# Result stores from ScalarE's queue, two late experts side by side on 128 partitions, and additions behind the last gated product

## What is computed

```python
def hierarchical_moe(h, ...):
    ...
    combine = ...          # (tokens, 16): the weights of each token's two experts, zero elsewhere
    gate = jnp.einsum('nd,edf->nef', h, w_gate)      # d = 1024, f = 512
    up = jnp.einsum('nd,edf->nef', h, w_up)
    act = jax.nn.silu(gate) * up * combine[..., None].astype(h.dtype)
    return jnp.einsum('nef,efd->nd', act, w_down)

def finish_layer(x, ...):
    ...
    y = hierarchical_moe(h, ...)
    return x + y.reshape(B, L, D)

y_prompt = rms_norm(xp, norm_final)
y_sample = rms_norm(xs, norm_final)
```

## Time and profile before

| | us |
|---|---|
| median of 3 runs | 888.52 (888.23 to 888.59) |
| the profiled execution, its own time | 887.74 |
| its span, first to last instruction | 886.1 |
| TensorE busy | 777.9 (88% of the span) |
| mean granted TensorE clock | 0.948 of full |
| DMA queue of SyncE | 154.16 MB |
| DMA queue of ScalarE | 5.86 MB |
| DMA queue of GpSimd | 10.30 MB |

### The profile page before, as it was taken

The page is one execution under the profiler, slowest core; times in us unless marked ns, Lnnn a source line. Parts: engine busy times, 40 slices in busy tenths (PEclk is TensorE's granted clock), DMA queues, the critical chain, the costliest instruction groups (busy, mean ns, idle before and its releaser), DMA issues.

```text
span 886.1 us, 12369 instructions
## 1 busy us (share of the span) xinstructions
PE 777.9 (88%) x4711; PEld 411.0 (46%) x4711; DVE 375.5 (42%) x869; ACT 224.4 (25%) x577; POOL 57.0 (6%) x87
## 2 busy tenths in 40 slices
PE   5988999999995889779788897799999999998457
PEld 2455465546544335345435464345455455554212
DVE  5421013571203655746755655373244333231062
ACT  1211110112202355565565641001010011100012
POOL 0111000200000000100000000200000000000220
PEclk9998999999996799999999999799999999999869
DMA  8256925173249600000000235886999999999832
GB/s 303 72 162 181 318 70 178 48 248 108 75 136 279 250 1 2 1 1 24 1 1 24 96 130 203 264 315 228 367 397 385 392 383 386 381 390 393 309 122 97
DMA packets 86381, 171.13 MB, mean 193 GB/s; under 512 B 9978, under 2 KB 25562, under 8 KB 86290
## 3 DMA queue, kind: packets, MB, share of 16 engines
q1 hardware_dynamic: 77698, 154.16, 49.1%
q0 software_dynamic: 3296, 10.30, 3.4%
q10 hardware_dynamic: 5328, 5.86, 1.9%
HBM read 151.00 MB, written 21.39 MB: 195 GB/s over the span
## 4 chain that ended last, share of the span: by engine, by line
PE 55%; issue 9%; DVE 7%; ACT 6%; DMA 3%; POOLq 0%; POOL 0%; ACTq 0%; DVEq 0%
PE bank L2294 15%; PE bank L2730 7%; PE bank L1685 6%; PE bank L2285 5%; PE bank L1620 4%; PE bank L2712 3%; PE bank L2328 3%; ACT reg L1116 3%; PE bank L1639 2%; DVE st L1277 2%; PE bank L2421 2%; ACT work L2584 1%; PE bank L2417 1%; PE bank L1622 1%; PE bank L1666 1%
## 5 line engine op out<-in xcount | busy, mean ns | idle before, releaser
L2730 PE MATMUL bank<-reg 128*128 128x512 f32 (+1 forms) x384 | 167.1, 581 | 2.5 <-DVE work L1233 1.3
L2294 PE MATMUL bank<-reg,qreg 128*32 128x128 f32 (+2 forms) x960 | 116.6, 363 | 3.8 <-DMA reg<-w_gate 1.9
L2730 PEld LDWEIGHTS bank<-reg 128*128 128x128 f32 x384 | 72.4, 197 | 72.1 <-issue 68.8
L2294 PEld LDWEIGHTS bank<-reg,qreg 128*32 128x32 f32 (+2 forms) x960 | 63.4, 132 | 53.8 <-issue 40.6
L1685 PE MATMUL bank<-reg 128*128 128x512 f32 (+1 forms) x160 | 81.8, 622 | 0.0
L2712 PE MATMUL bank<-cf,reg 128*128 128x128 f32 (+1 forms) x384 | 61.5, 287 | 18.6 <-DVE reg L2659 9.6
L2712 PEld LDWEIGHTS bank<-cf,reg 128*128 128x128 f32 (+1 forms) x384 | 43.2, 145 | 39.3 <-issue 29.9
L2584 ACT ACTIVATE work<-bank 128x128 f32<-128x128 f32 (+6 forms) x123 | 46.3, 417 | 49.5 <-PE bank L2712 27.5
L1639 PE MATMUL bank<-work,vreg 128*64 128x128 f32 x480 | 39.3, 295 | 12.7 <-ACT work L2584 11.9
L2285 PE MATMUL bank<-reg,work 128*128 128x512 f32 x112 | 49.5, 595 | 0.0
L1277 DVE TENSOR_REDUCE st<-bank 128x1 f32<-128x128 f32 (+3 forms) x64 | 28.4, 484 | 29.7 <-PE bank L1622 29.6
(11 more groups left out here) (338 smaller groups left out, 944.9 us busy)
## 6 DMA issues: line engine op xcount, KB each, us to landing
reg<-w_gate SPq DMA_DIRECT2D x12, 2048.0 KB, 19.4
reg<-w_up SPq DMA_DIRECT2D x12, 2048.0 KB, 21.1
reg<-w_down SPq DMA_DIRECT2D x12, 2048.0 KB, 15.0
reg<-w_in SPq DMA_DIRECT2D x4, 2048.0 KB, 9.3
expert_rows<-vreg SPq DMA_DIRECT2D x11, 512.0 KB, 5.2
reg<-cache_sb_k SPq DMA_DIRECT2D x16, 256.0 KB, 2.9
reg<-cache_sb_v SPq DMA_DIRECT2D x16, 256.0 KB, 3.0
qreg<-w_up SPq DMA_DIRECT2D x2, 2048.0 KB, 16.5
```

The costliest lines, as they stand in the source:

```text
L2294: ins = T.matmul(bank[which][rows, at_:at_ + w], rowsT[b][:, k, r0:r0 + n], w_[:, k, h * w:(h + 1) * w], start=(k == 0), stop=(k == KD - 1))
L2730: ins = nc.tensor.matmul(at("m", ("proj", n))[:, 0:w], hT[:, k, i * P:(i + 1) * P], win[:, pos % 2, k, 0:w], start=(k == 0), stop=(k == KD ...
```

## The change

The sizes of the turns are reordered (the same numbers in another order, turns 14 and 15 still with 64 rows), and `LATE` goes from 13 to 14: turn 13, now with 128 rows, goes through DRAM, turns 14 and 15 stay. Their down products are no longer split into side-by-side column groups: each fills 64 partitions (turn 14 the lower, turn 15 the upper) of bank 2 and bank 6 at full width, and ScalarE copies both banks to one tile `y_late`. So each token tile needs one pick matrix of 128 rows and two matmuls in place of six in the final product. `store_rows` moves from SyncE's order to the end of each turn in ScalarE's order, and is issued from ScalarE's queue. All `add_rows` come after `gated(15)`. One zero store of 64 rows goes (the late rows are 128 now), the pick matrices have 128 columns in place of 192, one transpose and one copy in place of two and six. `pool.wait_ge(e_up)` ahead of the gathers of tile 2 goes, and TensorE's wait for `e_y_v` ahead of the final stage.

```diff
-SIZES = (P, P, 64, P, P, 32, 96, P, 64, P, 32, 96, P, 64, 64, 64)
+SIZES = (P, P, 32, P, P, 64, P, 64, 32, 96, 64, 96, P, P, 64, 64)
...
-LATE = 13
+LATE = 14
...
-        for row, n in ((LATE_ROW, P), (LATE_ROW + P, LATE_ROWS - P)):
-            sp.dma_start(y_dram[row:row + n, :], vsb[0:n, 0:2, :].rearrange("p a b -> p (a b)")).then_inc(sg["y_zero"], 16)
+        sp.dma_start(y_dram[LATE_ROW:LATE_ROW + P, :], vsb[:, 0:2, :].rearrange("p a b -> p (a b)")).then_inc(sg["y_zero"], 16)
...
-        n = (6, 4, 0, 2, 6)[i]
+        n = (4, 0, 6, 2, 4)[i]
...
                 load_chunk(sp, n, expert_reg[CHUNKS[n][1]])
-                if n >= RING and before == "down":
-                    store_rows(waiting.pop(0))
...
-            for j in waiting:
-                store_rows(j)
-
...
             for i in range(TILES):
-                if i == 2:
-                    pool.wait_ge(sg["e_up"], LATE + 2)
...
             def y_out(j):
                 act.wait_ge(sg["e_down"], j + 1)
-                if j >= 2:
+                if 2 <= j <= LATE:
                     act.wait_ge(sg[f"e_st{j % 2}"], stored(j - 2))
                 w = min(512, D * SIZES[j] // P)
-                A.copy(y_late[j - LATE] if j >= LATE else y_rows[j % 2][:, 0:w], bank[2][:, 0:w]).then_inc(sg["e_y_a"], 1)
+                if j < LATE:
+                    A.copy(y_rows[j % 2][:, 0:w], bank[2][:, 0:w]).then_inc(sg["e_y_a"], 1)
+                else:
+                    A.copy(y_late[late_half(j), 0:512], bank[2][late_half(j), :])
+                    A.copy(y_late[late_half(j), 512:D], bank[6][late_half(j), :]).then_inc(sg["e_y_a"], 1)
+
+            def store_rows(j):
+                b, row = j % 2, first_row(j)
+                if j >= LATE:
+                    return
+                act.wait_ge(sg["e_y_a"], j + 1)
+                act.wait_ge(sg["e_y_v"], large_to(j))
+                for r0, n in BLOCKS[SIZES[j]]:
+                    w = D * n // P
+                    for rows, h in column_groups(n):
+                        act.dma_start(y_dram[row + r0:row + r0 + n, w * h:w * h + w], y_rows[b][rows, 8 * r0:8 * r0 + w]
+                                     ).then_inc(sg[f"e_st{b}"], 16)
...
                 if j >= 1:
                     y_out(j - 1)
+                    store_rows(j - 1)
...
-                for q in range(3):
-                    src = bank[7][0:64, P:P + r] if q == 2 else bank[7][64 * q:64 * q + 64, 0:r]
-                    for h in range(2):
-                        ins = V.tensor_copy(late_pick(q, i)[64 * h:64 * h + 64, :], src)
-                ins.then_inc(sg["picked"], 1)
+                V.tensor_copy(late_pick(i), bank[7][:, 0:r]).then_inc(sg["picked"], 1)
...
-                if j == LAST - 1:
-                    add_rows(0)
-                    add_rows(1)
-            for i in range(2, TILES):
+            for i in range(TILES):
                 add_rows(i)
...
             def down_blocks(j, sem):
                 w_ = chunk("down", j)
+                if j >= LATE:
+                    for to, at_ in ((bank[2], 0), (bank[6], 512)):
+                        for k in range(FF // P):
+                            ins = T.matmul(to[late_half(j), :], actsT[j % 2][:, k % 2, 64 * (k // 2):64 * (k // 2) + 64],
+                                           w_[:, k, at_:at_ + 512], start=(k == 0), stop=(k == 3))
+                    ins.then_inc(sem, 1)
+                    return
...
-            pe.wait_ge(sg["e_y_v"], large_to(LAST))
             overflow(pe, more, lambda: pe.wait_ge(sg["v_added"], 1))
...
             for h in range(2):
-                if i == 3 and h == 0:
-                    pe.wait_ge(sg["e_y_a"], NE)
                 T.matmul(to[:, h, :], ident[0:r, 0:r], x[0:r, i, 512 * h:512 * h + 512], start=True, stop=False)
-            for q in range(3):
-                pe.wait_ge(sg["e_y_a"], LATE + q + 1)
-                for h in range(2):
-                    ins = T.matmul(to[:, h, :], late_pick(q, i)[64 * h:64 * h + 64, :], y_late[q][64 * h:64 * h + 64, :],
-                                   start=False, stop=(q == 2))
+            if i == 0:
+                pe.wait_ge(sg["e_y_a"], NE)
+            for h in range(2):
+                ins = T.matmul(to[:, h, :], late_pick(i), y_late[:, 512 * h:512 * h + 512], start=False, stop=True)
             ins.then_inc(sg["late_full"], 1)
```

More of the change, by code:

```diff
@@ L771, in body @@
     route_weights(QT - 1)
-    for name, by in (("const", 16), ("const_b", 16), ("gain_attn", 16), ("table_zero", 16), ("y_zero", 16 * EXTRA + 32), ("router_in", 80),
+    for name, by in (("const", 16), ("const_b", 16), ("gain_attn", 16), ("table_zero", 16), ("y_zero", 16 * EXTRA + 16), ("router_in", 80),
                      ("iota", 1), ("zero", 1), ("act_chain", 0), ("dve_chain", 0), ("pe_chain", 0)):
@@ L1764, in body @@
     y_more = work[:, 1024:2048]
-    y_late = [y_rows[1][:, 0:512], y_rows[0][:, 0:512], y_rows[1][:, 512:1024]]
+    y_late = y_rows[0]
     picks = [rt[:, 0:LATE_ROWS], vc[:, :, :].rearrange("p a b -> p (a b)")[:, 0:LATE_ROWS]]
@@ L1817, in column_groups, with late_pick, late_half @@
         return [(slice(n * h, n * h + n), h) for h in range(P // n)]
[L1819 to L1826, removed]
+    def late_pick(i):
+        return dead[:, i * P:i * P + ROWS[i]]
+    def late_half(j):
+        return slice(64 * (j - LATE), 64 * (j - LATE) + 64)
     def gathered_rows(i, k):
@@ L1884, in next_expert @@
                 expert_reg.append(sp.value_load(order_i[0:1, j:j + 1], min_val=0, max_val=NE - 1))
[L1886 to L1896, removed]
             for n in range(6, len(CHUNKS)):
@@ L2361, in turn_picks @@
                     pe.wait_ge(sg["picked"], i)
-                T.transpose(bank[7][:, 0:r], to[:, 0:P], ident[0:r, 0:r])
-                T.transpose(bank[7][0:64, P:P + r], to[:, P:LATE_ROWS], ident[0:r, 0:r]).then_inc(sg["picks_turned"], 1)
+                T.transpose(bank[7][:, 0:r], to, ident[0:r, 0:r]).then_inc(sg["picks_turned"], 1)
             acquire_all(pe)
```

## The result

The changed kernel takes 863.99 us (median of 4 runs, 863.77 to 864.47), the kernel before 888.56 (888.23 to 893.67) beside it: a ratio of 0.9711, 95% interval 0.9676 to 0.9747. It is 24.6 us faster; the forecast was 20.9 faster, at 867.6 us. 0.9711 of the 888.52 on record is 862.8, just under the range of 863.5 to 876. The profiled execution took 864.47 us, with a span of 862.6.

The account below looks back on a forecast made before the run. Bound by an end chain of weight stream, store, gather, addition, gated product, down product. Last down product ends at 842.5, tiles 17.2, norm and store 5.5: span 865.2; plus 1.64 and 0.78 gives 867.6 us, range 863.5 to 876.

Parts of the forecast that it names:

- The chain at the end: End of kernel: weight stream, store, gather, addition, gated product, down product in series; the 16 us TensorE hole closes.
- late products: Down products of turns 14 and 15 at full width: 6.9 us each in place of 3.6.
- The rate of the weight stream: Weight loads from chunk 13 on: 388 GB/s, the mean of the earlier stretches; gate weights of turn 12 land at 761.5.
- chunk 13: Weight chunk from whose issue the DMA engines are full: issued 3.4 us earlier, at 615.0 in place of 618.47.
- Rival (d): Weight stream: its rate is off by 2% either way, 4 us over 212; no separate chance given.
- the zero store: Near 97 us: one zero store of 256 KB less, worth 0 to 0.7 us, counted as nothing.
- The two small terms: Added to the span: 1.64 us for the execution's own time, 0.78 from that execution to the median.
- Stores on ScalarE's queue: Store of turn 13: issued at 819.6, lands 7 us later at 826.6, against 16.8 for SyncE's stores.
- Gathers beside the last weights: End of stream: gather from 826.8 shares bandwidth, delaying w_down of 15 from 832.1 to 835.6.
- (a): End: store lands in byte order behind the stream, at 836.6; span 868.6, about 871 us; chance 0.12.
- (b): Last down product: TensorE falls to half clock after a wait, losing 2 to 7 us, 870 to 875; chance 0.11.
- (c): ScalarE held at each store issue: 878 us at 8 us holds, gain gone from 9.5; chance 0.09.

Follow-up runs that it names:

- e9: Changed kernel plus one unused tile of 128 bytes in each partition, putting buffers where the kernel before had them: 867.42 us, ratio 0.9781.
- e3: Changed kernel with its stores put back on SyncE's queue: 863.44 us, ratio 0.972.
- e1: Kernel before with its stores issued from ScalarE's queue at the end of each turn: 881.76 us, ratio 0.9911.
- e4: Changed kernel with add_rows(0) and add_rows(1) put back ahead of gated(15): 875.32 us, ratio 0.9832.
- e12: Changed kernel with 32 idle one-column copies, each waited for, behind each turn's stores on ScalarE: 886.43 us, ratio 0.9998.
- e7: Changed kernel with the old order of SIZES, LATE = 14 kept: 867.01 us, ratio 0.9772.
- e8: Changed kernel with the down products of turns 14 and 15 side by side again, copied to the same y_late: 860.76 us, ratio 0.9663.
- e6: Kernel before with stores from ScalarE's queue and all additions behind gated(15): 881.56 us, ratio 0.9929.

## Why the prediction was right or wrong

**The chain at the end: right.** It named store, gather, addition, gated product, down product as the series and said that the change leaves the products. Store issued 817.68 (forecast 819.6), gather 825.00 (826.8), so 7.3 us from one to the other where I took 7; gated product done at 825 (829); late products 6.87 and 7.08 (6.9); down 15 ends at 839.80 (842.5); the span ends 22.8 us behind it (22.7). The last addition ends at 846.2; the final stage asks for its tile at 853.7, so cover was more than the 4 us I gave it. Down 15 started on ScalarE's copies (832.7), not on its weights (835.6 forecast): they had landed at 827.6.

**The rate of the weight stream: the term that was mis-sized.** "At 388 GB/s, my mean of the stretches" was taken over from the kernel before. The stream to gate 12, forecast at 146.5 us from the issue of chunk 13, took 141.7 (616.75 to 758.41): by the same sum 401 GB/s and not 388. That is 4.8 us gained, of which a chunk 13 issued 1.75 late gave back a part: 3.1 at gate 12, 2.9 at down 15, 2.6 in the span. The proof is e9: with the placement of the kernel before, the changed kernel takes 146.1 us for this stretch, and TensorE loses 5.3 us in turns 9 to 12 against "some 6 us" forecast, where the changed kernel lost 1.4. That its time of 867.42 us is the 867.6 forecast is partly luck: its profiled span was 863.8, not 865.2, with chunk 13 at 613.33 and not 615.0, and its median lay 1.8 above that execution. Rival (d), which had 2% of rate as an error of either sign, had the sign open, a size somewhat too small (146.5 against 141.7 is 3%) and no reason. The reason was in the change, as a table of constants with fewer columns, and not in the profile: of the fewer late rows I had priced only the zero store.

**The two small terms.** Own time over span was 1.87 us (1.64 taken). The median lay 0.48 under the profiled execution, where I added 0.78 because it had lain above it before; that is 1.3 us of the miss. Together: 2.6 - 0.2 + 1.3 = 3.6 us (rounded), the whole of 867.6 against 863.99. An offset from one execution to a median is noise and had no place in the sum.

**Stores on ScalarE's queue: right in the landing, wrong in what it was for.** I took 7 us and 6.6 were measured; on SyncE's queue it is 11.2 (e3), not the 16.8 that I compared with the earlier trace rows. But e3 has the same time without the move. Two things free the end: in the new order the last load is issued before the result of turn 13 exists, and TensorE's two late products cover what is left. I took the price of a store right behind two loads and didn't ask when in the new order the last one is issued, nor how much slack the additions had.

**Gathers beside the last weights: not seen.** I gave `w_down` of 15 a delay of 3.5 us. They landed at 827.6, against 832.1 forecast without the delay and 835.6 with it: the stream was faster and nearly empty when the gather came (376 GB/s in 820:825, 247 in 825:830), and no product waited for those weights. The mechanism is real where the gather comes early: e1.

**Rivals.** (a) fell: gather at 825.00, not 837. (b) fell: TensorE's waits were 1.4 and 1.05 us, and both products behind them ran at full clock; e4 and e12 show what a longer one does, and e12 that 1.43 us can be enough elsewhere. (c) fell by its condition, issues of 0.33 to 1.18 us, but its price was understated: e12 uses up the gain at a hold of 7.1 us, where I set the point at 9.5.

**What each part is worth.** Taken from the changed kernel (863.4 to 864.0): order of additions 12 us (e4), order of sizes about 3.6 (e7), placement 3.4 to 4.0 (e9), queue nothing in time, some 5 us of slack (e3). The full width costs about 3 by the medians (e8; its interval and that of the changed kernel overlap) and 5.4 from gather to final stage in the traces. The pieces that weren't tried alone, turn 13 through DRAM and the shorter final stage, are left with what lies between e6 (881.56) and the changed kernel, 17.6 us less 3.6 and about 3.7, some 10 us if they add; in this kernel not all parts do (e6). The five tiles of the final stage take 17.6 us in place of 23.3 (the changed kernel and e6), so 5.7 of them can be read off.

## What to carry to other kernels

Before pricing a part, ask what will stand in front of it in the new order and what will cover it: the queue of the last store, 5 us in the landing, didn't change the time while TensorE had two products to do meanwhile, and a gather that is free at the end of the stream costs 9 us inside it. A table that changes its size moves every buffer behind it: compare addresses, not only instructions, and put the homes of streamed data on a multiple of 256 bytes (shown here against 128 off it). Gains of parts measured alone (0.9% and 1.5% here) needn't add (0.7% together).

## What the runs showed of the hardware

**Placement in SBUF.** Moving all buffers behind one table by 128 bytes, from a multiple of 256, costs 3% of the rate of a full weight stream: 377 to 392 GB/s against 391 to 403 (e9 beside the changed kernel), at a DMA share of 1.04 to 1.05 in both. The Trainium skill has a rule for it (page "DMA: Bandwidth & Descriptors", section "How a descriptor splits into AXI transactions"): a descriptor that doesn't start on a 256-byte boundary fetches from the boundary below and pays for the bytes in between. The weight queue moved 148.64 MB in 75202 packets, 1977 bytes each on average. By the page a packet of 2048 bytes at 128 would need 68 beats of 32 bytes in place of 64, an estimate of 6% more; half of that was measured. The page speaks of what is read, while SBUF is the side that is written for the weights, so that it is this rule which acts here is argued, not shown. Which buffer carries the effect (six homes of weights, the results, or the rows fetched) wasn't separated.

**Gathers beside the stream.** 4.3 MB of gathered rows put the last weights back by 9.4 us (e1), close to the 11 us that the bytes need at 388 GB/s, though they come from GpSimd's queue and the weights from SyncE's.

**Queue of a store beside a full stream.** In the same kernel stores of 512 KB landed in 11.2 us (median) on the queue of the weight loads (e3) and in 6.7 on ScalarE's (changed kernel).

**Clock behind a wait.** A wait of 3.47 us of TensorE at the end was followed by a product of 10.00 us in place of 7.08 (e12), one of 3.86 by 5.03 in place of 3.65 (e12), one of 9.3 us, a transpose later, by 9.28 (e4). 1.40 and 1.05 us cost nothing in the changed kernel, where the granted clock stayed at 1.00; but 1.43 us in e12 was followed by 8.83 in place of about 7, with 0.54 and 0.61 granted in 704:706 and 706:708. The length of the wait alone doesn't tell.
